# One layer of a hybrid model and two of another on one core: scores between two weight units, transposed values, added squares

## The chip, the core and the metric

The kernel runs on one core of a Trainium2 chip. A core has a matrix engine (TensorE, PE in the rows), VectorE (DVE), ScalarE (ACT), GpSimd (POOL) and SyncE (SP), each with a queue of its own that is worked off in order; they wait for each other through semaphores. Weights come from device memory by DMA. The metric is the time of one execution in microseconds, the median of several runs; less is better.

## What is computed

Two blocks follow each other on 256 tokens of width 1024, everything in fp32. The first has a state-space mixer with a gated norm over two groups of 512 channels, a gated linear attention with a norm over 256 channels a head, cross attention and a gated MLP. The second puts 16 meta tokens in front (272 tokens) and has a stick-breaking attention layer with an MLP, then a recurrent layer with an MLP. The parts that the change touches:

```python
# norms of the first mixer: y over groups of 512 channels, o over heads of 256
y = rmsnorm(y.reshape(Bsz, S, G, SSD_D_INNER // G), norm_g.reshape(G, SSD_D_INNER // G))
o = rmsnorm(o, norm_g).reshape(Bsz, S, GLA_DV)

def _sb_block(q_blk, k, v, q_pos):            # stick-breaking attention, 16 heads of 64
    z = jnp.einsum('bhqd,bhkd->bhqk', q_blk, k).astype(jnp.float32) * (SB_HEAD_DIM ** -0.5)
    causal = k_pos[None, :] < q_pos[:, None]
    log_keep = jnp.where(causal, -jax.nn.softplus(z), 0.0)
    after = lax.cumsum(log_keep, axis=3, reverse=True) - log_keep
    w = jnp.where(causal, jnp.exp(jax.nn.log_sigmoid(z) + after), 0.0)
    return jnp.einsum('bhqk,bhkd->bhqd', w.astype(v.dtype), v)
```

## The kernel before

**Weights.** All weights stream through a ring of four slots in units of 128x1024. For each unit SyncE loads `raw`, ScalarE rounds it to the high part `whi` (`split_hi`), VectorE takes the rest as the low part `wlo` (`split_lo`), and TensorE multiplies both with the high and low part of the activations (`xh`, `xl`): three matmuls for each of eight blocks of 128 channels, 24 a unit (`unit`, lines 438 to 440). A slot's `whi` may be written when TensorE is done with the unit four earlier (`unit_done`), and `wlo` when `whi` is there. Results go to four PSUM banks `acc`, which must have been read (`evacuated`) before the unit four later.

**Queues.** The order of each engine is written out by hand. Nothing is moved by a scheduler: what stands behind a waiting instruction on its engine waits as well.

**Stick-breaking stage.** Two heads make a pair; there are eight pairs, p = 0 to 7, and a ninth set, the tails, for the 16 last queries of all heads. TensorE's loop runs m from 0 to 10. In iteration m it does `sb_after(m-3)` (products of the triangular matrix with the softplus parts `softh` and `softl`, which are added in PSUM), then for m < 8 the query unit 2m and the key unit 2m+1, then `sb_scores(m-1)`: queries by keys into one of two PSUM pairs `z` in the tile `mix`. For m = 8 to 10 a `token_pair` of two value units stands in the place of the query and key units: the activations are the stationary operand and the weights move, so that the values come out token by token; with 128, 128 and 16 tokens it is 72 matmuls. `tail_scores` follows at m = 9. VectorE does in iteration m: `soft_abs(m-2)` (`sp`), `soft_sum(m-2)` (`softp`), `query_rows(2m)` (`sqd`, with the split of the next weights), `soft_lo(m-2)` (`softl`), `key_rows(2m+1)` (`skT`, with a split). ScalarE: `soft_terms(m-2)` (exponential and logarithm on `sp`), `weights(m-3)` (exponential of `z` into `wT`, which frees `z` for the pair after next), `soft_hi(m-2)` (`softh`), two `split_hi`. `sb_scores(p)` waits for `wT_ready` p-1, that is for `weights(p-2)`, since they share `z`.

`token_scales` turns the norm's factors into a column `rtok`, by which `token_scaled` multiplies the values.

**Norms.** In the first mixer's loop over weight units, m = 0 to 59, TensorE sums squares over channels by a matmul with a constant matrix: `st_ssd` at m = 47 over two groups of four blocks, `st_gla0` and `st_gla1` at m = 52 and 54 over two heads of two blocks each. ScalarE makes the squares at m = 44, 45 (`y`) and 50, 51 (`o`).

## Time and profile before

| | us |
|---|---|
| median of three runs | 1232.21 (1231.43 to 1232.97) |
| profiled execution | 1231.64 |
| its span, first to last instruction | 1229.9 |
| TensorE matmuls busy | 1203.1 (98%) |
| VectorE busy | 843.3 (69%) |
| ScalarE busy | 672.1 (55%) |
| mean granted TensorE clock | 0.994 |

The profiled execution is 1.7 us longer than its span. Times in rows count from the span's start. Matmuls overlap, so the distance of two starts is what one costs, not its duration. "Idle" in brackets is how long the engine sat idle before the instruction and what ended that. A matmul in fp32 appears as two instructions.

### The profile page before, as it was taken

How to read it: one execution, taken by the hardware profiler on the slowest of the kernel's cores; microseconds unless marked ns; L12 is line 12 of the kernel's file. 1: busy time of each engine (PE TensorE's matmuls, PEld its weight loads, DVE VectorE, ACT ScalarE, POOL GpSimd, SP SyncE). 2: the span in 40 equal slices, each digit the busy share in tenths (PEclk: the TensorE clock that was granted, in tenths of full speed). 3: DMA queues.
4: the chain of work that ended last, by engine and by line, in shares of the span. 5: the costliest groups of instructions: out<-in, count | busy, mean ns of one | idle time of the engine just before them, and what ended most of it. 6: DMA issues, size and time to landing. Idle time of an engine off the chain costs nothing.

```text
span 1229.9 us, 25642 instructions
## 1 busy us (share of the span) xinstructions
PE 1203.1 (98%) x9675; PEld 1173.0 (95%) x9675; DVE 843.3 (69%) x1271; ACT 672.1 (55%) x1011; POOL 43.5 (4%) x61
## 2 busy tenths in 40 slices
PE   8999999999999999999999999999999999999996
PEld 7999899999999999999988999999999989999996
DVE  6987765888756877776666537666454898766553
ACT  6655545747435656655555326656543686665331
POOL 2002311100000000000100000000000000000000
PEclk9999999999999999999999899999999999999999
DMA  6565434575553565666544224655655536656661
GB/s 217 159 187 161 132 104 125 159 219 182 169 157 122 172 187 185 188 185 188 161 122 123 80 68 141 187 171 177 206 180 174 154 108 186 199 181 185 186 188 51
DMA packets 56776, 197.54 MB, mean 161 GB/s; under 512 B 7152, under 2 KB 9456, under 8 KB 56576
## 3 DMA queue, kind: packets, MB, share of 16 engines
q1 hardware_dynamic: 53856, 192.96, 51.5%
q10 hardware_dynamic: 2848, 3.56, 0.9%
q8 instruction: 52, 0.85, 0.3%
q14 instruction: 20, 0.16, 0.0%
HBM read 195.45 MB, written 1.05 MB: 160 GB/s over the span
## 4 chain that ended last, share of the span: by engine, by line
PE 84%; DVE 9%; ACT 4%; issue 2%; DMA 1%; POOL 0%; ACTq 0%; DVEq 0%; POOLq 0%; SPq 0%
PE acc L438 23%; PE acc L440 23%; PE acc L439 23%; DVE wlo L1486 3%; PE acc L483 2%; PE acc L484 2%; PE acc L485 2%; ACT whi L1017 2%; PE mix L828 1%; DVE sq L1514 1%; PE mix L734 1%; DMA hT<-xT 1%; PE mix L715 1%; PE mix L499 1%; PE mix L609 1%
## 5 line engine op out<-in xcount | busy, mean ns | idle before, releaser
L1017 ACT ACTIVATE whi<-raw 128x1024 fp32r<-128x1024 f32 x366 | 385.3, 1057 | 399.1 <-PE acc L440 345.6
L1486 DVE TENSOR_TENSOR wlo<-raw,whi 128x1024 fp32r<-128x1024 f32 x366 | 447.0, 1224 | 200.8 <-ACT whi L1017 200.3
L438 PE MATMUL acc<-xh,whi 128*128 128x256 f32 (+1 forms) x1664 | 475.1, 286 | 4.5 <-DVE wlo L1486 2.8
L440 PE MATMUL acc<-xh,wlo 128*128 128x256 f32 (+1 forms) x1664 | 471.5, 283 | 0.0
L439 PE MATMUL acc<-xl,whi 128*128 128x256 f32 (+1 forms) x1664 | 471.2, 283 | 0.0
L438 PEld LDWEIGHTS acc<-xh,whi 128*128 128x128 f32 x1664 | 314.1, 189 | 9.3 <-DVE wlo L1486 3.6
L440 PEld LDWEIGHTS acc<-xh,wlo 128*128 128x128 f32 x1664 | 314.5, 189 | 0.0
L439 PEld LDWEIGHTS acc<-xl,whi 128*128 128x128 f32 x1664 | 312.9, 188 | 0.3
L439 PE MATMUL acc<-hl,whi 128*128 128x256 f32 (+1 forms) x688 | 195.4, 284 | 0.0
L438 PE MATMUL acc<-hh,whi 128*128 128x256 f32 (+1 forms) x688 | 195.0, 283 | 0.0
L440 PE MATMUL acc<-hh,wlo 128*128 128x256 f32 (+1 forms) x688 | 194.7, 283 | 0.0
L440 PEld LDWEIGHTS acc<-hh,wlo 128*128 128x128 f32 x688 | 129.9, 189 | 0.0
L439 PEld LDWEIGHTS acc<-hl,whi 128*128 128x128 f32 x688 | 129.4, 188 | 0.0
L438 PEld LDWEIGHTS acc<-hh,whi 128*128 128x128 f32 x688 | 129.1, 188 | 0.0
L438 PE MATMUL acc<-yh,whi 128*128 128x256 f32 (+1 forms) x320 | 91.0, 284 | 3.0 <-DVE yl L2126 1.4
L440 PE MATMUL acc<-yh,wlo 128*128 128x256 f32 (+1 forms) x320 | 90.5, 283 | 0.0
L439 PE MATMUL acc<-yl,whi 128*128 128x256 f32 (+1 forms) x320 | 90.5, 283 | 0.0
L438 PEld LDWEIGHTS acc<-yh,whi 128*128 128x128 f32 x320 | 60.4, 189 | 4.1 <-DVE wlo L1486 3.6
L440 PEld LDWEIGHTS acc<-yh,wlo 128*128 128x128 f32 x320 | 60.5, 189 | 0.0
L439 PEld LDWEIGHTS acc<-yl,whi 128*128 128x128 f32 x320 | 60.1, 188 | 0.0
L2025 DVE SCALAR_TENSOR_TENSOR t<-acc,rstd 128x272 f32<-128x272 f32 (+1 forms) x64 | 27.7, 433 | 31.3 <-PE acc L440 30.8
L483 PE MATMUL acc<-whi,xh 128*128 128x256 f32 (+1 forms) x160 | 45.9, 287 | 0.5 <-DVE wlo L1486 0.5
(350 smaller groups left out, 1423.5 us busy)
## 6 DMA issues: line engine op xcount, KB each, us to landing
raw<-w SPq DMA_DIRECT2D x366, 512.0 KB, 3.6
hT<-xT ACTq DMA_DIRECT2D x2, 512.0 KB, 6.5
mem<-memT ACTq DMA_DIRECT2D x1, 1024.0 KB, 6.8
rgw<-w ACTq DMA_DIRECT2D x2, 512.0 KB, 4.7
out<-hT SPq DMA_DIRECT2D x8, 128.0 KB, 2.0
xdt<-wsmall ACTq DMA_DIRECT2D x1, 192.0 KB, 7.0
pr<-par ACTq DMA_DIRECT2D x1, 114.0 KB, 4.5
hT<-metaT ACTq DMA_DIRECT2D x1, 64.0 KB, 5.8
```

Of the source, the lines that this page charges most:

```text
L438: nc.tensor.matmul(dst, whi[:, slot, n, :], rh, start=first, stop=False)
L439: nc.tensor.matmul(dst, whi[:, slot, n, :], rl, start=False, stop=False)
L440: return nc.tensor.matmul(dst, wlo[:, slot, n, :], rh, start=False, stop=last)
L483: nc.tensor.matmul(dst, ah[:, k, at:at + n], whi[:, s:s + 2, k, :], start=k == 0, stop=False)
L484: nc.tensor.matmul(dst, ah[:, k, at:at + n], wlo[:, s:s + 2, k, :], start=False, stop=False)
L485: last = nc.tensor.matmul(dst, al[:, k, at:at + n], whi[:, s:s + 2, k, :], start=False, stop=k == KB - 1)
L499: last = nc.tensor.matmul(dst[:, 0:T], mean1024[:, :], x[:, 0:T], start=i == 0, stop=i == len(parts) - 1)
L609: last = nc.tensor.matmul(dst[:, 256 * i:256 * i + 256], khk[po:po + CHUNK, c // 2, P * h:P * h + P], vt[po:po + CHUNK, c // 2, 256 * h:25 ...
L715: last = nc.tensor.matmul(mix[:, h % 2, 256 * t:256 * t + 256], xqT[:, 2 * h + i, P * t:P * t + P], xkT[:, 2 * h + i, :], start=i == 0, st ...
L1017: act.activation(whi[:, j, :, :].rearrange("p k c -> p (k c)"), raw[:, j, :], ACT.Copy)\
L1486: dve.tensor_tensor(wlo[:, j, :, :].rearrange("p k c -> p (k c)"), raw[:, j, :], whi[:, j, :, :].rearrange("p k c -> p (k c)").bitcast(F32 ...
L2025: dve.scalar_tensor_tensor(out=t4[:, j, 0:T], in0=acc[:, j, 0:T], scalar=0.0, in1=rstd[:, 0:T], op0=ALU.max, op1=ALU.mult).then_inc(evacua ...
```

## The change

Four edits. In the stick-breaking loop of TensorE the scores of pair m-1 move from behind the key unit to between the query unit and the key unit. On VectorE `softl` moves ahead of the split of the query unit's ring slot. The values are no longer computed token by token: a `value_unit` is an ordinary unit of 24 matmuls over 272 tokens, VectorE multiplies its result by the norm's factor into `svT`, three transposes on TensorE (`values_by_token`) turn it, and ScalarE copies it out (`values_out`); `token_scales` goes. And the squares are added on VectorE before the constant matmul: two additions at m = 46 and one at m = 51, with a new semaphore `n_sums`; `st_ssd` has two matmuls in place of eight, `st_gla0` and `st_gla1` two in place of four.

```diff
-            pool.memset(sv[:, 2, :], 0.0).then_inc(sbzero, 1)
+            pool.memset(svT[:, :, T2:KPAD], 0.0).then_inc(sbzero, 1)
...
+                        pe.wait_ge(n_sums, 2)
                         for grp in range(2):
-                            for b in range(4):
-                                pe.wait_ge(n_sq, 4 * grp + b + 1)
-                                last = nc.tensor.matmul(dst[:, 256 * grp:256 * grp + 256], mean512[:, :],
-                                                        sq[:, 4 * grp + b, 0:T1], start=b == 0, stop=b == 3)
+                            last = nc.tensor.matmul(dst[:, 256 * grp:256 * grp + 256], mean512[:, :],
+                                                    sq[:, 4 * grp, 0:T1], start=True, stop=True)
                         last.then_inc(misc_ready, 1)
...
                         dst = misc_bank(f"st_gla{i}")
+                        pe.wait_ge(n_sums, 3)
                         for hd in range(2):
-                            for vb in range(2):
-                                b = 4 * i + 2 * hd + vb
-                                pe.wait_ge(n_sq, 8 + 2 * i + hd + 1)
-                                last = nc.tensor.matmul(dst[:, 256 * hd:256 * hd + 256], mean256[:, :], sq[:, b, 0:T1],
-                                                        start=vb == 0, stop=vb == 1)
+                            last = nc.tensor.matmul(dst[:, 256 * hd:256 * hd + 256], mean256[:, :],
+                                                    sq[:, 4 * i + 2 * hd, 0:T1], start=True, stop=True)
                         last.then_inc(misc_ready, 1)
...
-            def pair_units(m):
-                for i in range(2):
+            def pair_units(m, halves):
+                for i in halves:
                     if m + i == 0:
...
                         stream_stats("fin1", T1)
-                if m == 1:
-                    token_scales()
-            def token_scales():
-                dst = misc_bank("tok_sb")
-                pe.wait_ge(rstd_ready, 5)
-                for t, (at, n) in enumerate(tiles2):
-                    last = nc.tensor.matmul(dst[0:n, t:t + 1], rstd[:, at:at + n], ident[:, 0:1], start=t == 0, stop=True,
-                                            skip_group_check=True)
...
                 if p == 1:
-                    pe.wait_ge(misc_free, R["tok_sb"] + 1)
+                    pe.wait_ge(misc_free, R["st_fin1"] + 1)
                 if p >= 2:
...
                 dst = mix[:, 3 - p // 2, 256 * (p % 2):256 * (p % 2) + 256]
-                for j in range(2):
-                    pe.wait_ge(evacuated[2 * (p // 2 % 2) + j], OUTS["sv"] // 4 + p // 4 + 1)
+                pe.wait_ge(evacuated[p % 4], OUTS["sv"] // 4 + p // 4 + 1)
                 for h in range(2):
...
+            def value_unit(n):
+                unit("sv", n, n % 4, xh, xl, T2)
+            def values_by_token(n):
+                pe.wait_ge(svT_ready, n + 1)
+                for t in range(3):
+                    last = nc.tensor.transpose(acc[:, n % 4, P * t:P * t + P], svT[:, n % 2, P * t:P * t + P], ident[:, :])
+                last.then_inc(svt_done, 1)
...
                 if m < PAIRS:
-                    pair_units(m)
-                else:
-                    token_pair("sv", 2 * (m - PAIRS), xh, xl, tiles2)
+                    pair_units(m, (0,))
                 if 1 <= m <= PAIRS:
                     sb_scores(m - 1)
-                elif m == PAIRS + 1:
+                if m < PAIRS:
+                    pair_units(m, (1,))
+                else:
+                    n = 2 * (m - PAIRS)
+                    value_unit(n)
+                    if n:
+                        values_by_token(n - 1)
+                    value_unit(n + 1)
+                    values_by_token(n)
+                if m == PAIRS + 1:
                     tail_scores()
             sb_after(PAIRS)
+            values_by_token(5)
             for p in range(4):
...
             tail_out(0)
-            token_pair("sv", 6, xh, xl, tiles2)
+            value_unit(6)
+            value_unit(7)
+            values_by_token(6)
...
             so_part(0, 0, 6)
+            values_by_token(7)
...
+            def values_out(n):
+                act.wait_ge(svt_done, n + 1)
+                act.activation(sv[:, :, P * n:P * n + P], acc[:, n % 4, 0:3 * P].rearrange("p (t c) -> p t c", t=3),
+                               ACT.Copy).then_inc(evacuated[n % 4], 1)
...
                 soft_hi(m - 2)
-                sv_hi(2 * (m - PAIRS))
-                sv_hi(2 * (m - PAIRS) + 1)
+                n = 2 * (m - PAIRS)
+                sv_hi(n)
+                if n:
+                    values_out(n - 1)
+                sv_hi(n + 1)
+                values_out(n)
             weights(PAIRS)
+            values_out(5)
...
             sv_hi(7)
+            values_out(6)
+            values_out(7)
             pairs_out(3)
...
                             dve.tensor_tensor(y[:, b, :], y[:, b, :], sz[:, b, :], ALU.mult).then_inc(n_y, 1)
+                    if m == 46:
+                        dve.wait_ge(n_sq, 8)
+                        grouped = sq[:, :, 0:T1].rearrange("p (g b) t -> p g b t", g=2)
+                        dve.tensor_tensor(grouped[:, :, 0:2, :], grouped[:, :, 0:2, :], grouped[:, :, 2:4, :], ALU.add)\
+                            .then_inc(n_sums, 1)
+                        dve.wait_ge(n_sums, 1)
+                        dve.tensor_tensor(grouped[:, :, 0, :], grouped[:, :, 0, :], grouped[:, :, 1, :], ALU.add)\
+                            .then_inc(n_sums, 1)
+                    if m == 51:
+                        dve.wait_ge(n_sq, 12)
+                        paired = sq[:, :, 0:T1].rearrange("p (h b) t -> p h b t", h=4)
+                        dve.tensor_tensor(paired[:, :, 0, :], paired[:, :, 0, :], paired[:, :, 1, :], ALU.add)\
+                            .then_inc(n_sums, 1)
...
                                              in1=rstd[o_, :], op0=ALU.mult, op1=ALU.mult).then_inc(done, 1)
-                split_lo(UNITS["sqk"][0] + n + 4)
...
                     dve.wait_ge(sbzero, 4)
-                dve.wait_ge(unit_done, UNITS["sv"][0] + 2 * n + 2)
-                token_scaled(sv, 2 * n, (P, P, META))
-                split_lo(UNITS["sv"][0] + 2 * n + 4)
-                split_lo(UNITS["sv"][0] + 2 * n + 5)
+                if n >= 2:
+                    dve.wait_ge(svt_done, n - 1)
+                dve.wait_ge(unit_done, UNITS["sv"][0] + n + 1)
+                dve.tensor_tensor(svT[:, n % 2, 0:T2], acc[:, n % 4, 0:T2], rstd[:, :], ALU.mult).then_inc(svT_ready, 1)
+                split_lo(UNITS["sv"][0] + n + 4)
...
                     soft_lo(m - 2)
+                split_lo(UNITS["sqk"][0] + 2 * m + 4)
                 key_rows(2 * m + 1)
-                if m == 1:
-                    token_scales()
             for m in range(PAIRS, PAIRS + 3):
...
                 soft_lo(m - 2)
-                values(m - PAIRS)
+                values(2 * (m - PAIRS))
+                values(2 * (m - PAIRS) + 1)
                 if m == PAIRS:
...
             tails_lo(0)
-            values(3)
+            values(6)
+            values(7)
             pairs_lo(3)
```

On TensorE around the scores of pair 5, before (L438 to L440 are the matmuls of a weight unit, L813 to L819 the scores, L840 to L848 `sb_after`):

```order
3767 L439 MATMUL acc<-xl,whi 128x272
3768 L440 MATMUL acc<-xh,wlo 128x272
3769 L813 MATMUL mix<-sqd,skT 128x512 [waits evacuated3,wT_ready,evacuated2,sqd_ready]
3770 L815 MATMUL mix<-sqd,skT 128x256
3771 L817 MATMUL mix<-cmask,identb 128x2x128
3772 L819 MATMUL mix<-cmask,identb 128x256
3773 L840 MATMUL mix<-softh,ntri 128x512 [waits softl_ready]
3774 L842 MATMUL mix<-softh,nones 128x2x128
```

and of the change, where they are L440 to L442, L801 to L807 and L828 to L836:

```order
3740 L441 MATMUL acc<-xl,whi 128x272
3741 L442 MATMUL acc<-xh,wlo 128x272
3742 L801 MATMUL mix<-sqd,skT 128x512 [waits evacuated3,wT_ready,evacuated2,sqd_ready]
3743 L803 MATMUL mix<-sqd,skT 128x256
3744 L805 MATMUL mix<-cmask,identb 128x2x128
3745 L807 MATMUL mix<-cmask,identb 128x256
3746 L440 MATMUL acc<-xh,whi 128x272 [waits evacuated1,lo_ready]
```

The scores have moved ahead of the key unit, with the same waits, and `sb_after` of the next iteration no longer follows on them.

On TensorE at the end of the last key unit, the scores of pair 7, before (L483 to L485 are the last matmuls of a token pair):

```order
3907 L484 MATMUL acc<-wlo,xh 16x256
3908 L485 MATMUL acc<-whi,xl 16x256
3909 L813 MATMUL mix<-sqd,skT 128x512 [waits evacuated3,wT_ready,evacuated2,sqd_ready]
3910 L815 MATMUL mix<-sqd,skT 128x256
3911 L817 MATMUL mix<-cmask,identb 128x2x128
```

and of the change:

```order
3827 L442 MATMUL acc<-xh,wlo 128x272
3828 L828 MATMUL mix<-softh,ntri 128x512 [waits softl_ready]
3829 L830 MATMUL mix<-softh,nones 128x2x128
3830 L836 MATMUL mix<-softh,ntri 128x256
3831 L828 MATMUL mix<-softl,ntri 128x512
3832 L830 MATMUL mix<-softl,nones 128x2x128
3833 L836 MATMUL mix<-softl,ntri 128x256
3834 L801 MATMUL mix<-sqd,skT 128x512 [waits evacuated3,wT_ready,evacuated2,sqd_ready]
3835 L803 MATMUL mix<-sqd,skT 128x256
```

The scores of pair 7 stood behind a token pair; now they stand directly behind `sb_after(5)`.

On VectorE in one iteration of the same loop, before:

```order
599 L1957 TENSOR_SCALAR sp<-mix 128x768 [waits head_ready]
600 L1963 SCALAR_TENSOR_TENSOR softp<-mix,sp 128x768 [waits sb_act]
601 L1944 SCALAR_TENSOR_TENSOR sqd<-acc,rstd 64x272 [waits unit_done]
602 L1944 SCALAR_TENSOR_TENSOR sqd<-acc,rstd 64x272
603 L1486 TENSOR_TENSOR wlo<-raw,whi 128x1024 [waits hi_ready]
604 L1968 TENSOR_TENSOR softl<-softp,softh 128x768 [waits softh_ready]
605 L1951 TENSOR_TENSOR skT<-acc,rstd 128x272 [waits unit_done]
606 L1486 TENSOR_TENSOR wlo<-raw,whi 128x1024 [waits hi_ready]
```

and of the change:

```order
600 L1980 TENSOR_SCALAR sp<-mix 128x768 [waits head_ready]
601 L1986 SCALAR_TENSOR_TENSOR softp<-mix,sp 128x768 [waits sb_act]
602 L1968 SCALAR_TENSOR_TENSOR sqd<-acc,rstd 64x272 [waits unit_done]
603 L1968 SCALAR_TENSOR_TENSOR sqd<-acc,rstd 64x272
604 L1991 TENSOR_TENSOR softl<-softp,softh 128x768 [waits softh_ready]
605 L1506 TENSOR_TENSOR wlo<-raw,whi 128x1024 [waits hi_ready]
606 L1974 TENSOR_TENSOR skT<-acc,rstd 128x272 [waits unit_done]
607 L1506 TENSOR_TENSOR wlo<-raw,whi 128x1024 [waits hi_ready]
```

`softl` and the first of the two splits have changed places.

## Rows read from the trace of the kernel before

**Rows 1.** The page, part 1: busy time, share of the span, instructions of each engine.

```profile
PE 1203.1 (98%) x9675; PEld 1173.0 (95%) x9675; DVE 843.3 (69%) x1271; ACT 672.1 (55%) x1011; POOL 43.5 (4%) x61
```

**Rows 2.** Timeline of TensorE, one round: start, duration, instruction, [idle before].

```profile
626.68 0.50 PE L840 MATMUL mix<-softh,ntri 128*128 128x512 f32 x1 [0.42 <-DVE softl L1968]
...
627.73 0.28 PE L438 MATMUL acc<-xh,whi 128*128 128x272 f32 x1
...
633.77 1.02 PE L813 MATMUL mix<-sqd,skT 128*128 128x512 f32 x2
...
635.85 0.51 PE L840 MATMUL mix<-softh,ntri 128*128 128x512 f32 x1 [0.41 <-DVE softl L1968]
```

**Rows 3.** Timeline of VectorE, from one `sp` to the next.

```profile
637.32 0.95 DVE L1957 TENSOR_SCALAR sp<-mix 128x768 uint32<-128x768 uint32 x1
640.06 0.96 DVE L1963 SCALAR_TENSOR_TENSOR softp<-mix,sp 128x768 f32<-128x768 f32 x1 [1.79 <-ACT sp L1312]
...
645.36 1.22 DVE L1486 TENSOR_TENSOR wlo<-raw,whi 128x1024 fp32r<-128x1024 f32 x1
646.49 0.95 DVE L1957 TENSOR_SCALAR sp<-mix 128x768 uint32<-128x768 uint32 x1
```

**Rows 4.** Timeline of ScalarE in the same round.

```profile
639.93 0.80 ACT L1322 ACTIVATE wT<-mix 128x768 f32<-128x768 f32 x1
```

**Rows 5.** Timeline of TensorE at the end of key unit 3, m = 1.

```profile
616.36 0.63 PE L796 MATMUL mix<-ident,rstd 128*128 128x1 f32 x6
616.92 1.12 PE L813 MATMUL mix<-sqd,skT 128*128 128x512 f32 x2
...
618.45 0.37 PE L438 MATMUL acc<-xh,whi 128*128 128x272 f32 x1
```

**Rows 6.** Timeline of VectorE there.

```profile
616.56 0.44 DVE L1951 TENSOR_TENSOR skT<-acc,rstd 128x272 f32<-128x272 f32 x1 [0.65 <-PE acc L440]
617.71 1.23 DVE L1486 TENSOR_TENSOR wlo<-raw,whi 128x1024 fp32r<-128x1024 f32 x1 [0.71 <-ACT whi L1017]
```

**Rows 7.** Timeline of ScalarE there.

```profile
616.62 1.06 ACT L1017 ACTIVATE whi<-raw 128x1024 fp32r<-128x1024 f32 x1 [1.97 <-PE acc L440]
```

**Rows 8.** Timeline of TensorE: ends of a token pair's neighbours, and a pair's start.

```profile
684.31 0.28 PE L848 MATMUL mix<-softl,ntri 128*128 128x256 f32 x1
...
692.92 7.71 PE L828 MATMUL mix<-sqd,skT 128*128 128x32 f32 x48
...
702.35 0.41 PE L483 MATMUL acc<-whi,xh 128*128 128x256 f32 x1
```

**Rows 9.** Timeline of TensorE in the first mixer: eight transposes.

```profile
84.73 1.04 PE L556 MATMUL mix<-ident,xc 128*128 128x128 f32 x8
```

**Rows 10.** Timeline of VectorE at m = 8.

```profile
678.63 0.96 DVE L1968 TENSOR_TENSOR softl<-softp,softh 128x768 fp32r<-128x768 f32 x1 [0.91 <-ACT softh L1318]
...
685.71 1.73 DVE L1924 RECIPROCAL rstdh<-rtf 128x256 f32<-128x256 f32 x1
```

**Rows 11.** Timeline of TensorE at `st_ssd` (L680) and `st_gla1` (L691).

```profile
188.51 3.61 PE L680 MATMUL mix<-sq,mean 128*128 128x256 f32 x16
191.77 0.47 PE L438 MATMUL acc<-xh,whi 128*128 128x256 f32 x1
...
219.12 1.99 PE L691 MATMUL mix<-sq,mean 128*128 128x256 f32 x8 [0.90 <-ACT khk L1199]
```

**Rows 12.** Timeline of VectorE at m = 46.

```profile
187.02 1.23 DVE L1486 TENSOR_TENSOR wlo<-raw,whi 128x1024 fp32r<-128x1024 f32 x1 [0.72 <-ACT whi L1017]
```

**Rows 13.** Timeline of ScalarE at m = 51.

```profile
209.65 1.13 ACT L1194 ACTIVATE sq<-xdt 128x512 f32<-128x512 f32 x2
```

**Rows 14.** Stretches: busy us of each engine, granted clock, DMA share, GB/s.

```profile
694.00:696.00 2.00, 2.00 (x20) 2.00 (x19) 2.00 (x3) 1.18 (x2) 0.00 (x0) 0.93 0.00 0
705.00:706.00 1.00, 1.00 (x7) 1.00 (x7) 0.51 (x1) 0.46 (x1) 0.00 (x0) 0.52 0.00 0
1224.00:1226.00 2.00, 0.00 (x0) 0.00 (x0) 2.00 (x6) 0.00 (x0) 0.00 (x0) 0.70 0.39 134
```

More of the change, by code:

```diff
@@ L94 @@
         "st_gla0", "st_gla1", "st_mem", "st_xattn", "pt0", "pt1", "pt2", "pt3",
[1 row of a table removed]
+        "st_ffn", "st_sb", "st_fin1", "st_mlp0", "st_lru", "st_mlp1", "st_fin2"]
 R = {name: n for n, name in enumerate(MISC)}
@@ L258, in blocks_kernel @@
         sv = sb("sv", [P, 3, D], stack=s4)
+        svT = sb("svT", [P, 2, KPAD], stack=s4)
         sp = sb("sp", [P, ZC], stack=s4)
@@ L308, in blocks_kernel @@
         n_sq, n_r, n_y, o_step = sem("n_sq"), sem("n_r"), sem("n_y"), sem("o_step")
+        n_sums = sem("n_sums")
         yh_ready, yl_ready, merged = sem("yh_ready"), sem("yl_ready"), sem("merged")
@@ L316, in blocks_kernel @@
         tail_done, sqd_ready = sem("tail_done"), sem("sqd_ready")
-        tok_ready = sem("tok_ready")
+        svT_ready, svt_done = sem("svT_ready"), sem("svt_done")
         both_ready, meta_ready, metah_ready, metal_ready, metasq_ready, sqb_ready, sumb_ready = [sem(n) for n in
@@ L515, in operand @@
                 return xl_ready, KB * OPER[norm]
-            tiles1, tiles2 = [(0, P), (P, P)], [(0, P), (P, P), (2 * P, META)]
+            tiles1 = [(0, P), (P, P)]
             def small_products():
@@ L787, in pair_units @@
                         stream_stats("fin1", T1)
-                if m == 1:
-                    token_scales()
-            def token_scales():
-                dst = misc_bank("tok_sb")
-                pe.wait_ge(rstd_ready, 5)
-                for t, (at, n) in enumerate(tiles2):
-                    last = nc.tensor.matmul(dst[0:n, t:t + 1], rstd[:, at:at + n], ident[:, 0:1], start=t == 0, stop=True,
-                                            skip_group_check=True)
-                last.then_inc(misc_ready, 1)
             def sb_scores(p):
@@ L1561, in token_scaled @@
                 c = 128 * m
-                if len(tiles) == 3:
-                    dve.tensor_scalar(dst[0:META, 2, c:c + 256], acc[0:META, m % 4, 256:512], rtok[0:META, 2:3], None,
-                                      ALU.mult)
                 for t in range(2):
@@ L1926, in stream_rms @@
                 dve.wait_ge(rstd_ready, norms[0])
-            def token_scales():
-                dve.wait_ge(misc_ready, R["tok_sb"] + 1)
-                dve.tensor_copy(rtok[:, 0:2], mix[:, MISCB, 0:2]).then_inc(tok_ready, 1)
-                dve.tensor_copy(rtok[0:META, 2:3], mix[0:META, MISCB, 2:3]).then_inc(misc_free, 1)
             inverse_rms("sb", T2)
```

1 row of the table MISC is left out of this document.

## The prediction

> **What bounds the kernel now.** I read the page first: TensorE is busy in 98% of the span [rows 1], so the time is what TensorE has to issue, plus the little it waits. A part that only frees VectorE or ScalarE changes nothing until it ends a TensorE wait, and a part that makes TensorE wait costs its whole length. Then I read the timeline of TensorE through the stick-breaking stage. In rounds m = 3 to 7 it repeats every 9.17 us [rows 2]: `sb_after(m-3)` takes 1.05 us (626.68 to 627.73), two weight units take 6.04 us (627.73 to 633.77), the scores follow, and then TensorE waits 0.41 us for `softl`. The scores cost 1.53 us of issue (616.92 to 618.45, [rows 5]). So TensorE has 1.05 + 6.04 + 1.53 = 8.62 us of work in a round. The 0.41 to 0.43 us wait stands six times in this stage. Last I read VectorE and ScalarE in the same rounds [rows 3, 4], because both serve the weight splits and the softplus in one queue each, and the edit reorders who waits for whom.
>
> **Where the scores stand, and what they need.** `sb_scores(m-1)` overwrites the PSUM pair that `weights(m-3)` reads, so it waits for `wT_ready`. In ScalarE's queue `weights(m-3)` stands behind the two softplus steps of pair m-2, and these wait for `soft_abs(m-2)`, which stands in VectorE's queue behind `key_rows(2m-1)` and its weight split. Now there are two units (6.04 us) between `sb_after(m-3)` and the scores. `sp` starts at 637.32 [rows 3], `wT` starts at 639.93 and takes 0.80 [rows 4]: it is ready 3.41 us after `sp` starts, at 640.73. `sb_after` started at 635.85 [rows 2] and with one unit behind it would be through at 635.85 + 1.05 + 3.02 = 639.92, earlier than 640.73. The second unit is what hides `wT` today; the change takes it out of that place and puts it behind the scores.
>
> **The new round.** A loop closes that was open before: `sp` of a pair, `wT` (3.41 us), scores (0.06 to wake TensorE, 1.53), key unit (3.02), its evacuation `skT`, the split of the next weights, next `sp`. The end of that loop has its own rows: TensorE leaves the key unit at 616.36 [rows 5], `skT` starts at 616.56 (0.20 later), and the split waits for ScalarE's `whi`, which itself may start only when this unit is done (616.62, [rows 7]); so `wlo` starts at 617.71, 1.15 after `skT` [rows 6]. From the split to the next `sp` it is 1.13 (645.36 to 646.49, [rows 3]). Sum: 3.41 + 0.06 + 1.53 + 3.02 + 0.20 + 1.15 + 1.13 = **10.50 us** a round, against 8.62 us of TensorE work. TensorE then waits 1.88 us before the scores of pairs 2 to 6: **+9.4 us** in five rounds. The low part of softplus ahead of the weight split does what it says: five of the six waits for `softl` go, 5 x 0.42 = **-2.1 us** (the first round, where nothing has fallen behind yet, keeps its own). But `softl` isn't on the new loop, and so it can't shorten it.
>
> **The scores of pair 7.** In iteration m = 8 there is no query unit, and the scores follow directly on `sb_after(5)`. Before, a pair of value units of 8.4 us stood between. Count from the end of the last key unit: 0.20 + 1.15 + 1.13 to `sp`, 3.41 to `wT`, 0.06: 5.95 us, of which `sb_after(5)` covers 1.05. TensorE waits **+4.9 us**.
>
> **Values.** A token pair costs 684.31 + 0.12 to 692.92, 8.49 us [rows 8], for 72 matmuls. In its place: two units (6.04) and six transposes. Eight transposes take 1.04 us [rows 9], 0.13 each, so 0.78. Saved 8.49 - 6.04 - 0.78 = 1.67 a pair, four pairs: **-6.7 us**. ScalarE gets eight copies of 128x384 out of PSUM, each below the 0.80 that `wT` takes for 768 columns [rows 4], and VectorE loses its twelve token scalings for eight multiplications of the kind of `skT`, 0.44 [rows 6]; both engines have idle time there (0.91 of it stands in [rows 10]), and I cost them at nothing. Without that cover it would be 0.5 us a copy, 4 us at most. But `values_by_token(2)` stands right behind unit 3 and ahead of the tail scores, and its `svT` comes on VectorE behind `softl` of pair 7. From the end of value unit 1: TensorE has 0.33 + 1.05 + 3.02 + 0.33 + 3.02 = 7.75 us to do. VectorE has evacuation and split (0.20 + 1.15 + 1.13), the reciprocal of 1.73 [rows 10], `sp` to `softp` 2.74 (637.32 to 640.06, [rows 3]), `softp` to `softl` 1.87 (0.96 and then 0.91 of waiting for `softh`, [rows 3, 10]), `softl` 0.93, the multiplication 0.44, the wake-up 0.06: 10.25. TensorE waits **+2.5 us**. `token_scales` goes, with 616.36 to 616.92: **-0.6 us** [rows 5].
>
> **Added squares.** `st_ssd` drops from 16 instructions in 3.26 us (188.51 to 191.77, [rows 11]) to 4, 0.85 us. But the two additions start on VectorE after the split that starts at 187.02 [rows 12]: 1.13 + 1.25 + 0.70, so the sums are there at 190.1 and TensorE waits 1.6 us. The first adds 1024 columns as the split does (1.23), the second half of that. 0.85 + 1.6 in place of 3.26: -0.8. At `st_gla0` four instructions go (-0.8), but it now waits for ScalarE's squares of m = 51, whose pair starts at 209.65 and takes 1.13 [rows 13], and for 1.2 us of VectorE behind: ready at 212.1, while TensorE got there at 210.65; +0.7 net. `st_gla1` keeps its 0.90 wait for ScalarE [rows 11] and loses 0.8. Together **-0.8 us**; bounds -3.5 (if no sum is waited for) and +1.
>
> **TensorE's clock.** The granted clock was halved once in the middle of the run: it goes down in 694 to 696 and comes back in 705 to 706 [rows 14]. Ahead of the fall stood the tail scores, matmuls of 32 columns, since 692.92. It also fell at the end: matmuls had stopped by 1221.4, and within 1224 to 1226 the mean is 0.70 [rows 14]. The first of these stretches stays, since the tail scores do. The 4.9 us wait is new and holds no matmul at all, so I expect a second low stretch behind it. Before, dense matmuls ran from 702.35 [rows 8] to about 705.9 at half clock before it was lifted, 3.6 us in which half was lost: **+1.8 us**. Bounds 0 (no fall) and 3.6 (twice as long, or the fall ahead of the tail scores earlier as well, since 2.5 us of waiting now stand before them).
> The Trainium skill, TensorE: Matmul & The Clock Gate, section "HAM oscillation", says that an array left idle in a wait between bursts is throttled again and starts the next burst cold. The end of this trace agrees (1224 to 1226 above). By that rule the term is there; by a reading in which only sparse matmuls, as the tail scores, bring the fall it would be 0 and the time 1.8 us lower.
>
> **Sum.** +9.4 + 4.9 + 2.5 - 2.1 - 6.7 - 0.6 - 0.8 = +6.6, with the clock +1.8: **+8.4 us**. The profiled execution took 1231.64 us (span 1229.9 and 1.7 around it), so 1240.0 by its own time; the median of the runs shown, 1232.21, is 0.6 above it: **1240.6 us**.
>
> **Rivals.** (A) The round is not closed as I say: weights are ready when the scores need them, and TensorE stays the only bound. Then the waits are not there and 6.7 + 2.5 + 0.6 + 0.8 = 10.6 us go: 1221.6 us, faster. For it: TensorE's share of 98%, and the instruction count falls. Against it: the 3.41 us of [rows 3, 4] and the order of the queues, both plain. It decides where `wT` of pair m-3 is ready less than 4.07 us after `sb_after(m-3)` starts. Chance 0.08. (B) The waits are there, but about 60% as large, since a round starts from a VectorE that had slack (a shorter `sp`-to-`wT` step or a split that finds its `whi` early); 16.8 x 0.6 = 10.1 of waits against 10.2 saved: 1232 us. Chance 0.07. (C) The clock: a second and a longer first low stretch, 3.6 us in place of 1.8, and each wait 10% longer (1.7), since every switch between kinds of matmul costs about 0.1: 8.4 + 3.5 = 11.9, 1244.1 us. Chance 0.15. The forecast holds 0.70, from 1237.0 (waits 10% shorter, no second fall) to 1242.5.
>
> **Range and chances.** 1235 to 1244.5 leaves out A, most of B and the far end of C. A measurement of this kernel can tell about 0.2% (2.5 us) from no change. Faster than 1229.7: A and a little of B, 0.09. Within: the rest of B, 0.06. Slower: 0.85.
>
> **What would show it.** Right: in the timeline, rounds of 10.5 us between the `sp` instructions; TensorE's first score matmul with 1.9 us of idle released by ScalarE's `wT`, five times, and once 4.9 us; no idle ahead of `sb_after` but in the first round; 2.5 us ahead of the third group of transposes, released by `svT`; a second low stretch of the clock behind the 4.9 us. TensorE's busy time falls by about 10 us while the span grows. Wrong: rounds of 8.6 us (A); a wait for `wT` well under 1 us (B); a clock that stays full behind the long wait takes 1.8 off. The squares are wrong if TensorE reaches `st_ssd` after the second addition, which would make them -3 alone.

## The result and the profile after

The changed kernel takes **1244.44 us** (median of 5 runs, 1244.09 to 1245.14) against 1232.21 (1231.43 to 1232.97): ratio 1.0103, 95% interval 1.0089 to 1.0117. It is slower, as forecast, but by 12.2 us and not by 8.4. The profiled execution took 1244.44, with a span of 1242.7. Page and list of waits of the changed kernel, TensorE's rows; a wait's columns are us in total, times, longest:

```profile
PE 1198.7 (96%) x9577; PEld 1169.3 (94%) x9577; DVE 845.5 (68%) x1268; ACT 675.6 (54%) x1019; POOL 41.5 (3%) x61
```

TensorE does less work than in [rows 1] and is busy for a smaller share of a longer span. But its busy time fell by 4.4 us only, where the forecast had about 10: matmuls at a low clock are busy for longer. Where it waits:

```profile
PE mix L801 <- ACT wT L1330: 14.6, 6, 4.9
PE acc L872 <- DVE svT L2001: 2.5, 1, 2.5
PE mix L681 <- DVE sq L1765: 1.6, 1, 1.6
PE mix L690 <- DVE sq L1770: 1.4, 1, 1.4
PE mix L828 <- DVE softl L1991: 0.4, 1, 0.4
```

The first row is the new one: six waits ahead of the scores, five of about 1.9 us and one of 4.9, all released by ScalarE's `wT`. The last one is what is left of the six waits of [rows 2]. Timelines of one round at the full clock, TensorE, then VectorE and ScalarE (start, duration, instruction, idle before and its releaser); they answer to [rows 2, 3, 4]:

```profile
643.58 1.10 PE L801 MATMUL mix<-sqd,skT 128*128 128x512 f32 x2 [1.92 <-ACT wT L1330]
...
648.20 0.39 PE L828 MATMUL mix<-softh,ntri 128*128 128x512 f32 x1
...
654.24 1.10 PE L801 MATMUL mix<-sqd,skT 128*128 128x512 f32 x2 [1.92 <-ACT wT L1330]
```

```profile
648.40 0.44 DVE L1974 TENSOR_TENSOR skT<-acc,rstd 128x272 f32<-128x272 f32 x1 [1.59 <-PE acc L442]
649.55 1.23 DVE L1506 TENSOR_TENSOR wlo<-raw,whi 128x1024 fp32r<-128x1024 f32 x1 [0.71 <-ACT whi L1025]
650.69 0.95 DVE L1980 TENSOR_SCALAR sp<-mix 128x768 uint32<-128x768 uint32 x1
653.43 0.96 DVE L1986 SCALAR_TENSOR_TENSOR softp<-mix,sp 128x768 f32<-128x768 f32 x1 [1.78 <-ACT sp L1320]
```

```profile
651.68 0.84 ACT L1318 ACTIVATE sp<-sp 128x768 f32<-128x768 f32 x1 [2.16 <-DVE sp L1980]
652.55 0.84 ACT L1320 ACTIVATE sp<-sp 128x768 f32<-128x768 f32 x1
653.30 0.79 ACT L1330 ACTIVATE wT<-mix 128x768 f32<-128x768 f32 x1
```

This is the loop of the forecast, closed: the key unit ends at 648.20, `skT` follows at 648.40, the split at 649.55, `sp` at 650.69, `wT` ends at 654.09, and the scores that follow start at 654.24. The round is 654.24 - 643.58 = 10.66 us (forecast 10.50; 9.17 before). Of the 0.16 too little, 0.09 is the step from the end of `wT` to the scores (0.15 us, forecast 0.06) and 0.07 is scores and key unit (643.58 to 648.20, 4.62 us, forecast 4.55).

What the forecast had too small is the clock. The granted clock has two levels in these rows, full (1.00) and half (0.50); a value between is a stretch that held both. Stretches of the changed kernel from one pair's scores to the next (us, TensorE busy with its count, granted clock, DMA share, GB/s):

```profile
631.34:643.58 12.24, 10.32 (x61) 0.86 0.34 97
643.58:654.24 10.66, 8.74 (x61) 1.00 0.33 100
654.24:664.90 10.66, 8.74 (x60) 1.00 0.33 98
664.90:677.09 12.19, 10.27 (x61) 0.86 0.28 88
677.09:687.74 10.65, 5.72 (x36) 0.95 0.35 98
687.74:698.33 10.59, 10.59 (x58) 0.73 0.01 2
708.72:717.21 8.49, 8.49 (x52) 0.61 0.47 125
```

Of the first four rows two are 1.6 and 1.5 us longer than the others, with the same instructions and nearly the same wait (2.00 against 1.92 us at 631.34), and these two have a mean clock of 0.86. The sixth row is the stretch behind the 4.9 us wait, the last one the tail scores. The scores and the two units behind that wait take 10.34 us:

```profile
687.74 2.05 PE L801 MATMUL mix<-sqd,skT 128*128 128x512 f32 x2 [4.93 <-ACT wT L1330]
...
698.08 0.49 PE L872 MATMUL acc<-ident,svT 128*128 128x128 f32 x3
```

The low clock at the tail scores isn't new. It is the same in both traces, 13 us of which have a mean clock of 0.61 (before, then after); in the changed kernel it only starts earlier against them:

```profile
694.00:707.00 13.00, 13.00 (x73) 0.61 0.25 81
709.00:722.00 13.00, 13.00 (x72) 0.61 0.30 82
```

Both traces cut at the same instructions (the first matmul of `sb_after`, and the end of the span):

| stretch | before | after | difference | forecast |
|---|---|---|---|---|
| start to m = 3 (squares, token scales) | 626.68 | 625.11 | -1.6 | -1.4 |
| m = 3 to m = 8, five rounds | 45.87 | 56.60 | +10.7 | +7.3 |
| m = 8 to m = 9 (pair 7, first values) | 10.86 | 16.62 | +5.8 | +5.0 |
| m = 9 to m = 10 (values, tail scores) | 17.09 | 18.88 | +1.8 | +0.8 |
| m = 10 to the end (two pairs of values) | 529.40 | 525.49 | -3.9 | -3.3 |
| sum | 1229.9 | 1242.7 | +12.8 | +8.4 |

The tail scores took 7.58 us before (692.92 to 700.50, clock 0.69) and take 8.49 now, and the units behind them lose as much less: 0.9 us of the last two differences has only moved from the last row to the one above it.

### The profile page after: what moved, and what is told of

It is laid out like the page before. It is cut to its first block, busy times and chain, and to the rows that moved or that the text cites. A ratio compares the mean times of both kernels' runs of the same rounds, so it can differ in the third digit from the quotient of the medians.

```text
span 1242.7 us, 25454 instructions
## 1 busy us (share of the span) xinstructions
PE 1198.7 (96%) x9577; PEld 1169.3 (94%) x9577; DVE 845.5 (68%) x1268; ACT 675.6 (54%) x1019; POOL 41.5 (3%) x61
## 4 chain that ended last, share of the span: by engine, by line
PE 84%; DVE 8%; ACT 5%; issue 2%; DMA 1%; POOL 0%; ACTq 0%; DVEq 0%; POOLq 0%; SPq 0%
PE acc L440 24%; PE acc L442 24%; PE acc L441 24%; DVE wlo L1506 3%; ACT whi L1025 2%; PE acc L485 1%; PE acc L486 1%; PE acc L487 1%; PE mix L801 1%; PE mix L816 1%; DVE sq L1534 1%; PE mix L733 1%; DVE sp L1980 1%; PE mix L714 1%; ACT sp L1318 1%
## 5 line engine op out<-in xcount | busy, mean ns | idle before, releaser
L440 PE MATMUL acc<-xh,whi 128*128 128x256 f32 (+1 forms) x1728 | 496.6, 287 | 3.6 <-DVE wlo L1506 1.9
L442 PE MATMUL acc<-xh,wlo 128*128 128x256 f32 (+1 forms) x1728 | 491.5, 284 | 0.0
L441 PE MATMUL acc<-xl,whi 128*128 128x256 f32 (+1 forms) x1728 | 491.4, 284 | 0.0
L440 PEld LDWEIGHTS acc<-xh,whi 128*128 128x128 f32 x1728 | 328.3, 190 | 8.7 <-DVE wlo L1506 2.7
L442 PEld LDWEIGHTS acc<-xh,wlo 128*128 128x128 f32 x1728 | 328.3, 190 | 0.0
L441 PEld LDWEIGHTS acc<-xl,whi 128*128 128x128 f32 x1728 | 327.0, 189 | 0.3
L440 PE MATMUL acc<-hh,whi 128*128 128x256 f32 (+1 forms) x688 | 195.0, 283 | 0.0
L442 PE MATMUL acc<-hh,wlo 128*128 128x256 f32 (+1 forms) x688 | 194.7, 283 | 0.0
L442 PEld LDWEIGHTS acc<-hh,wlo 128*128 128x128 f32 x688 | 129.9, 189 | 0.0
L440 PEld LDWEIGHTS acc<-hh,whi 128*128 128x128 f32 x688 | 129.1, 188 | 0.0
L440 PE MATMUL acc<-yh,whi 128*128 128x256 f32 (+1 forms) x320 | 91.2, 285 | 3.1 <-DVE yl L2151 1.4
L442 PE MATMUL acc<-yh,wlo 128*128 128x256 f32 (+1 forms) x320 | 90.5, 283 | 0.0
L440 PEld LDWEIGHTS acc<-yh,whi 128*128 128x128 f32 x320 | 60.4, 189 | 4.2 <-DVE wlo L1506 3.6
L442 PEld LDWEIGHTS acc<-yh,wlo 128*128 128x128 f32 x320 | 60.5, 189 | 0.0
L1396 ACT ACTIVATE hh<-t 128x272 f32 (+1 forms) x64 | 27.2, 426 | 8.4
```

What stands on the lines that cost most here:

```text
L440: nc.tensor.matmul(dst, whi[:, slot, n, :], rh, start=first, stop=False)
L441: nc.tensor.matmul(dst, whi[:, slot, n, :], rl, start=False, stop=False)
L442: return nc.tensor.matmul(dst, wlo[:, slot, n, :], rh, start=False, stop=last)
L1396: act.activation(blk(hh, 4 * i + j, 0, T), t4[:, j, 0:T], ACT.Copy).then_inc(hh_ready, 1)
```

## The experiments

Each edit is made to the kernel that its heading or text names. Each time is the median of four or more executions, but for one, which is named; each trace is of one execution.

**1. The order undone.** The changed kernel, its scores behind both units again:

```diff
                 if m < PAIRS:
-                    pair_units(m, (0,))
-                if 1 <= m <= PAIRS:
-                    sb_scores(m - 1)
-                if m < PAIRS:
-                    pair_units(m, (1,))
+                    pair_units(m, (0, 1))
                 else:
...
+                if 1 <= m <= PAIRS:
+                    sb_scores(m - 1)
                 if m == PAIRS + 1:
                     tail_scores()
```

> The changed kernel with one part undone: the scores of a head pair stand again behind both weight units of their round. My theory is that this order alone made the loss, by a loop (scores, DVE's softplus chain, ScalarE's order, weights, next scores) and by the low clock behind its waits. Then the 14.6 us in which PE waits for wT ahead of mix and the low clock stretches in the rounds (about 6 us) go, what is left is the gain of the other parts: 1232.2 less 2.1 (wait for softl), 6.7 (values), 0.6 (token scales), 0.8 (squares), and about 1.0 back for a wait ahead of the transposes of value block 2, so about 1223, round of 8.6 to 8.7 us. Rival: the extra low clock comes from the value units and their transposes, not from the waits; then it stays and the time is about 1228. Second rival: the softplus chain itself has become longer by the earlier softl, then a round stays over 10 us and the time stays at 1240 or more.

Measured: **1220.99 us** (1220.46 to 1223.91), ratio to before 0.9917 (0.9904 to 0.9931). Wherever TensorE stands in the stage, it is now this (list of waits), and from 600 to 680 us the clock is full:

```profile
PE acc L872 <- DVE svT L1999: 0.9, 1, 0.9
```

```profile
600.00:680.00 80.00, 79.19 (x567) 1.00 0.45 133
```

On top of the other edits the order costs 1244.4 - 1221.0 = 23.4 us; without it the rest of the change is a gain of 11.2.

**2. The order alone**, in the kernel before (the same lines the other way round).

> The kernel before with one part of the change alone: the scores of a pair between the two weight units. By the loop, a round takes 10.66 us as in the changed kernel, against 9.04 before: five of them, +8.1. The wait ahead of the scores of pair 7 is 4.9, and the low clock stretches of the rounds cost about 6: 1232.2 + 8.1 + 4.9 + 6 = 1251, worse than the whole change. If the clock is not the waits' doing, 1245. Rival: the order is harmless by itself and becomes harmful only with the earlier softl or the value units (ScalarE's copies): then 1232 to 1235.

Measured: **1250.88 us** (1248.33 to 1251.20), ratio 1.0148 (1.0133 to 1.0164); forecast 1251. Its list of waits:

```profile
PE mix L813 <- ACT wT L1324: 13.4, 6, 4.9
PE mix L840 <- DVE softl L1970: 2.6, 1, 2.6
```

The loop needs neither the earlier `softl` nor the value units. From one `sb_after` to the next its rounds take 9.63, 12.31, 10.64, 12.20 and 10.66 us, so here too two of five have low clock:

```profile
638.15:650.46 12.31, 10.39 (x63) 0.86 0.35 120
650.46:661.10 10.64, 8.72 (x62) 1.00 0.20 54
```

In the kernel before, the order costs 18.7 us, 4.7 less than in experiment 1. About that much (4.2, experiment 5) is what the earlier `softl` is worth where the loop is open: behind the closed loop the round is 10.66 with it and without it. The rival that makes it harmless by itself is out by 16 us.

**3. The loop opened on ScalarE.** The changed kernel with its order of scores:

```diff
-                if m >= 2:
-                    soft_terms(m - 2)
                 if m >= 3:
                     weights(m - 3)
+                if m >= 2:
+                    soft_terms(m - 2)
```

> The changed kernel, with its order of scores, and one change on ScalarE alone: the weights of a pair (wT) are formed ahead of the softplus terms of the next pair. If the loop is what makes PE wait, and ScalarE's order is what closes it, the waits of 1.92 us ahead of the scores of pairs 2 to 6 go, the 4.93 us one ahead of pair 7 falls to about 1, and the clock falls no more often than before: 1244.4 - 9.6 - 3.9 - 6 = 1225, round of 8.6 to 8.8 us. Rival: DVE's chain of a pair (sp, softp, softl) is the limit, not ScalarE's order: then the waits only move to softl and the time stays within 3 us of 1244.

Measured: **1226.14 us** (1223.68 to 1228.20), ratio 0.9946 (0.9932 to 0.9960); forecast 1225. List of waits, and three rounds (the two calls change places in the loop for m = 8 to 10 as well):

```profile
PE mix L801 <- ACT wT L1330: 1.1, 1, 1.1
```

```profile
637.39:645.88 8.49, 8.49 (x63) 1.00 0.37 120
645.88:654.37 8.49, 8.49 (x62) 1.00 0.42 123
654.37:662.87 8.50, 8.50 (x63) 1.00 0.40 127
```

Two exchanged calls on an engine that is busy 54% of the time take 18 us off. The rounds have the full clock. At the tail scores this execution (1228.2, the slowest of the five) has more low clock than the kernel before, where it was 0.61 over 13 us; the expectation had excluded that:

```profile
688.00:704.00 16.00, 16.00 (x84) 0.57 0.23 67
```

The experiment shows that the link of the loop is ScalarE's queue, where `weights(m-3)` stood behind softplus steps that it doesn't need; VectorE's chain isn't the limit. It also gives TensorE's work in a round without a wait: 8.49 us, where the forecast had 8.62.

**4. TensorE kept busy in its waits.** The changed kernel, with matmuls whose result the next unit of the bank overwrites:

```diff
+            def filler(count, j, turns):
+                pe.wait_ge(evacuated[j], turns)
+                for n in range(count):
+                    nc.tensor.matmul(acc[:, j, 0:256], nones[:, :], xh[:, 0, 0:256], start=True, stop=True)
             def sb_scores(p):
+                if p == PAIRS - 1:
+                    filler(36, 0, OUTS["sv"] // 4)
+                elif p >= 2:
+                    filler(13, (2 * p + 3) % 4, (OUTS["sqk"] + 2 * p + 3) // 4)
...
+                    if n == 2:
+                        filler(17, 0, OUTS["sv"] // 4 + 1)
                     values_by_token(n)
```

> The changed kernel with matmuls added whose result nobody reads (they are overwritten by the next unit of their bank): 13 ahead of the scores of each of pairs 2 to 6, 36 ahead of those of pair 7, 17 ahead of the transposes of value block 2, each of 256 columns, 0.12 us apart. They fill the time in which PE waits there and change nothing else, so the waits' length in time stays and PE is busy in them. If the low clock stretches in the rounds come from PE standing still, they go and their cost with them: 1244.4 - 6 = 1238.4, granted clock of 1.00 through the five rounds, each 10.66 us. If the clock has another cause, the stretches stay and the time is 1244.4 or, with fillers that run over at the low clock, up to 1246.

Measured: **1237.70 us** (1236.44 to 1240.92), ratio 1.0057 (1.0043 to 1.0071). Four rounds, and the timeline at one of their waits:

```profile
632.40:643.07 10.67, 10.28 (x73) 1.00 0.37 109
643.07:653.72 10.65, 10.28 (x73) 1.00 0.31 98
653.72:664.38 10.66, 10.28 (x73) 1.00 0.32 100
664.38:675.05 10.67, 10.29 (x74) 1.00 0.35 99
```

```profile
653.72 1.10 PE L811 MATMUL mix<-sqd,skT 128*128 128x512 f32 x2 [0.37 <-ACT wT L1342]
```

The rounds keep their 10.66 us, as the loop wants it, and every one of them is at 1.00. More work by 118 matmuls, and 6.7 us less time. The rival with another cause of the clock had 1244.4 or more. So the waits without matmuls are the cause of the low clock in the rounds. The 6.7 isn't its price alone, though. Against the trace of the change the five rounds take 3.1 us less (53.5) and the stage with pair 7 2.7 less (13.93): 5.8 behind the waits. The stage with the tail scores is 2.9 shorter as well, since the low clock is shorter there (mean 0.89 from 698 to 714, against 0.61 over 13 us), and the stretch up to m = 3 is 1.1 longer; the execution in the trace is the fastest of the five, 1236.44.

**5. to 7. The other parts alone**, each in the kernel before: `softl` ahead of the split, the values by channel without token scales, the added squares. The second and third take their hunks from the diff of the change; of each the core:

```diff
                                              in1=rstd[o_, :], op0=ALU.mult, op1=ALU.mult).then_inc(done, 1)
-                split_lo(UNITS["sqk"][0] + n + 4)
...
                     soft_lo(m - 2)
+                split_lo(UNITS["sqk"][0] + 2 * m + 4)
                 key_rows(2 * m + 1)
```

```diff
-                    token_pair("sv", 2 * (m - PAIRS), xh, xl, tiles2)
+                    n = 2 * (m - PAIRS)
+                    value_unit(n)
+                    if n:
+                        values_by_token(n - 1)
+                    value_unit(n + 1)
+                    values_by_token(n)
```

```diff
+                        pe.wait_ge(n_sums, 2)
                         for grp in range(2):
...
+                            last = nc.tensor.matmul(dst[:, 256 * grp:256 * grp + 256], mean512[:, :],
+                                                    sq[:, 4 * grp, 0:T1], start=True, stop=True)
```

> The kernel before with one part of the change alone: on DVE the low part of softplus (softl) stands ahead of the split of the first weight unit's low part. PE waited six times 0.42 us for softl, 2.5 in all. My theory: these waits go and nothing else becomes late, 1232.2 - 2.5 = 1229.7. Rival: the split that now stands behind softl comes late for its unit (a wait ahead of the first unit of a round), or the waits are taken up by a stretch of low clock that starts elsewhere: then 1232.

> The kernel before with one part of the change alone: the values formed by channel in eight units, scaled on DVE and transposed on PE, and the token scales gone. By the sum of the forecast a pair of values costs 6.82 instead of 8.49 (four pairs, -6.7), the token scales 0.6, and a wait of about 1 us stands ahead of the transposes of value block 2, as in the run with the order undone, where it was 0.90: 1232.2 - 6.7 - 0.6 + 1.0 = 1225.9. Rival: the gain in the values is smaller than the sum says and part of what the run with the order undone gained came from softl or the squares: then 1228 or more.

> The kernel before with one part of the change alone: the squares of the statistics added on DVE, so that PE multiplies a quarter (SSD) and a half (GLA) as often. The sum: PE's 3.61 us become 1.10 behind a wait of 1.6, its two of 1.9 become 1.10 each, one behind a wait of 1.4 in place of the one of 0.9 the other had: -0.8, 1231.4. Rival: PE's waits are longer than the work saved, because DVE takes up the adding at a time at which it is itself late: 1232.5 or more. It is near what five rounds can tell; the trace with its waits must decide.

Measured: `softl` alone **1227.69 us** (1226.39 to 1229.02), ratio 0.9964 (0.9951 to 0.9978); values alone **1225.78** (1225.06 to 1227.05), 0.9953 (0.9940 to 0.9967); squares alone **1230.69** (1229.76 to 1232.00), 0.9991 (0.9982 to 1.0000). Against their 1231.86 of before these are -4.2, -6.1 and -1.2, together -11.4: the 11.2 that experiment 1 left. The squares are at the edge of what the runs tell; their two waits stand in the trace as forecast, 1.6 and 1.4.

`softl` brought more than the 2.5 us of its waits. The timeline of the kernel before, from the last score matmul to the wait, and of this kernel at the same place and a round later, say why:

```profile
635.17 0.27 PE L819 MATMUL mix<-cmask,identb 128*128 128x256 bf16 x1
635.85 0.51 PE L840 MATMUL mix<-softh,ntri 128*128 128x512 f32 x1 [0.41 <-DVE softl L1968]
```

```profile
635.22 0.27 PE L819 MATMUL mix<-cmask,identb 128*128 128x256 bf16 x1
635.24 0.48 PE L840 MATMUL mix<-softh,ntri 128*128 128x512 f32 x1
...
643.74 0.48 PE L840 MATMUL mix<-softh,ntri 128*128 128x512 f32 x1
```

Without a wait a matmul starts while the one ahead of it is still running, here 0.02 us behind its start. With the wait it starts 0.68 behind. The shown idle time of 0.41 leaves out the overlap that is lost. The round agrees: 643.74 - 635.24 = 8.50 us in place of 9.17. Six such waits are 6 x 0.68 = 4.1 us, the measured 4.2.

**8. The tail scores woven into value units**, on the kernel of experiment 1 (one product of 32 columns, `tail_scores(1)`, behind each product of the second half of unit 3 and the first half of unit 4):

```diff
+            def woven_unit(n, first, stop):
...
+                for k in range(KB):
+                    if first <= k < stop and len(tail_products) == 3 * PAIRS:
+                        pe.wait_ge(wT_ready, PAIRS - 1)
...
+                        if first <= k < stop:
+                            tail_scores(1)
```

> Built on the changed kernel with the order of scores undone (1221.0): the 24 products of the tail scores no longer stand in one row but one behind each of 12 products in the second half of value unit 3 and of 12 in the first half of value unit 4. In the run with the order undone they took 8.5 us, most of it at a granted clock of 0.50, and the softplus terms behind them made nobody wait. Theory: the clock falls there since PE has only these small products to do for several us; woven between full products it stays at 1.00 and the 4.9 us lost to the low clock in that stretch go, as does the 0.9 us wait ahead of them: 1216 with a second wait of up to 1 for the low part of the last softplus. Rival: the clock falls all the same, because the small products are as many and only spread: then 1220 to 1221, and since the last softplus chain starts no earlier, a wait of 2 to 4 us ahead of its use makes it 1223.

Measured: **1218.57 us** (1215.80 to 1218.88), ratio 0.9887 (0.9871 to 0.9902). Two stretches of experiment 1, then the same of this kernel:

```profile
686.00:696.00 10.00, 10.00 (x50) 0.53 0.35 107
706.00:716.00 10.00, 10.00 (x96) 1.00 0.16 54
```

```profile
686.00:696.00 10.00, 10.00 (x85) 1.00 0.35 107
706.00:716.00 10.00, 10.00 (x72) 0.83 0.00 0
```

The same small products no longer bring the clock down where they are spread between full ones:

```profile
682.96 0.37 PE L880 MATMUL acc<-xl,whi 128*128 128x272 f32 x1
683.17 0.30 PE L817 MATMUL mix<-sqd,skT 128*128 128x32 f32 x2
```

But it falls later, behind the next row of small products (the tails' outputs), so that only half of the expected gain arrived, 2.4 us.

**9. and 10. Late sums, and woven outputs.** On the kernel of 8, `st_ssd`, `st_gla0` and `st_gla1` in the middle of the next weight unit; and on that, the outputs of the tails between the products of value unit 6:

```diff
+            middle = {48: ssd_sums, 53: lambda: gla_sums(0), 55: lambda: gla_sums(1)}
...
-                        unit(phase, n, n % 4, xh, xl, T1)
+                        unit(phase, n, n % 4, xh, xl, T1, mid=middle.get(m))
```

```diff
-            tail_out(0)
-            value_unit(6)
+            unit_with(6, out_piece)
```

> The kernel with the woven tail scores (1218.6), with one more edit: PE multiplies the added squares not at the end of weight units 47, 52 and 54, but in the middle of units 48, 53 and 55, 1.5 us later, while DVE is adding. PE's waits of 1.6 and 1.4 us ahead of these products were all that kept the added squares from being worth their saved work. Theory: both go and nobody else comes late, since DVE's reciprocal behind the first one starts some 4 us behind the products: 1218.6 - 3.0 = 1215.6. Rival: ScalarE, which takes the roots ahead of its weight splits, stands 1.5 us longer and PE waits for the next weight unit instead: 1218.6 or a little more.

> The kernel of the run beside it, and in addition the 18 products of 32 columns that make the tails of the first six pairs are woven one by one between the products of value unit 6, where they stood in one row of 4.4 us, behind which the granted clock was 0.87 and 0.79 in two stretches of 5 us (1.7 us lost). Theory: the clock stays up, -1.7, and their own time stays: 1213.9 if the late sums bring their 3.0. Rival: this low stretch comes from the pairs' own products ahead of them (64 columns wide in the weights) and stays, or the readers of the tails come later and make PE wait: no gain over the run beside it.

> The kernel with the woven tail scores and the late sums once more, for a look alone. Its profiled execution took 1217.8 us and had a low granted clock from 705 to 720 us worth about 3.4 us, while four executions without a profile took 1212.8 to 1214.8. If this low stretch comes in some executions and not in others, this look shows either 1213 to 1214 with a clock of 1.00 there, or again 1217 to 1218 with the stretch. If it comes in all of them and the difference is the profiler's, a time near 1217.8 with the stretch says nothing new, and a time near 1213 with the stretch in it speaks against the clock as the cause.

Measured: late sums **1213.22 us** (1212.82 to 1217.79), ratio 0.9849 (0.9836 to 0.9862); with woven outputs **1213.31** (1212.88 to 1214.21), 0.9850 (0.9836 to 0.9863); a single further execution of the first of the two 1217.03. The late sums brought 5.4 us where 3.0 were expected: besides the waits of 1.6 and 1.4, the 0.9 ahead of `st_gla1` went as well, and one of 0.4 came:

```profile
PE mix L624 <- ACT kt L1135: 0.4, 1, 0.4
```

That is 3.5 us of shown waits. The remaining 2 us are within the spread of the two kernels. By the medians the second edit brought nothing. By the traces it did what it should (the first row is late sums, the second with woven outputs), while both profiled executions of the first have the low stretch and take 1217 to 1218:

```profile
706.00:716.00 10.00, 10.00 (x58) 0.66 0.00 0
```

```profile
706.00:716.00 10.00, 10.00 (x83) 1.00 0.30 78
```

That isn't the only difference between the two. Late sums have a second low stretch near the start of the execution (first row), woven outputs have none there (second row), and the edits don't reach that place:

```profile
14.00:20.00 6.00, 4.69 (x25) 0.72 0.61 229
14.00:20.00 6.00, 4.30 (x32) 1.00 0.51 179
```

Of the 4.9 us between these two traces, 3.2 stand behind the last `sb_after` and 1.7 ahead of m = 3. A low stretch at 14 to 20 us stands in 7 of the 13 traces, a place that no edit here reaches: in those of experiments 4 to 9 and of the further execution.

My reading is that each of these stretches comes in some executions of the kernel of late sums and not in others, since four without a profile took 1212.8 to 1214.8; no trace of such a short execution exists, so it stays open. The woven outputs spread over 1.3 us and the late sums over 5; with five executions each it isn't shown that the weave did this. Both are 18.8 to 18.9 us, 1.5%, faster than the kernel before, and 31 faster than the change.

## Why the prediction was wrong in its size

**Right: the loop.** Five waits of 1.92 to 2.00 us (forecast 1.88), a round of 10.66 (10.50), released by `wT`; closed by ScalarE's order (experiment 3) and by nothing else in the change (experiments 1 and 2). **Right: pair 7**, 4.93 us against 4.9; **the wait for `svT`**, 2.5 against 2.5; the squares' 1.6; the one wait for `softl` that stays. **Right: the gains.** Values and token scales, less the wait of the value transposes: -6.1 alone. The squares -1.2 alone, forecast -0.8 (its own three parts add up to -0.9). The -2.1 for `softl` holds only as a part of the sum, which counts the new waits from 8.62 us of work; by itself it is worth 4.2 without the loop, and next to nothing with it.

**Wrong: the step "TensorE's clock"**, a term of +1.8 with bounds of 0 and 3.6. It counted one new low stretch, behind the wait of 4.9 us, and put the bound at twice that. I had costed the five waits of 1.9 us at their length alone. Two of the rounds that hold them have a clock of 0.86: 12.43 and 12.18 us from one `sb_after` to the next against 10.66, +1.8 and +1.5. Behind the long wait the scores and two units took 10.34 us where they take 1.50 + 6.04 at the full clock: +2.8, so that the one stretch that was counted was sized too low as well. Together 6.1 by the trace; in experiment 4, with matmuls in the waits, these stages are 5.8 shorter. This is 4.3 us more than the term and above its upper bound. It takes the time to the very end of the range (1244.44 by the median, just inside 1244.5; 1244.9 by the ratio, just outside).

**Wrong and hidden: two terms that nearly cancel.** The round was 0.16 us longer than forecast, +0.8 in five. The work of a round was taken as 8.62 plus a wait of 0.42, 9.04, where [rows 2] show 9.17 from one to the next (-0.7). By experiments 3 and 5 these 9.17 are 8.49 of work and 0.68 for the wait: a wait costs about 0.25 us more than its shown idle time. The parts outside the rounds came out within 0.3 us of their terms each, and as their sum, once the 0.9 that only moved is set off. 4.3 + 0.8 - 0.7 = 4.4, what lies between forecast and trace.

**The rivals.** A (no waits) and B (60% of them) are out by the waits alone. C had the cause in part and the time nearly, 1244.1, but this is luck: it had a longer first stretch and waits 10% longer, where the first stretch stayed as long as before, the waits came out as forecast, and new stretches stood in the rounds.

## What to carry to other kernels

Before moving an operation forward on one engine, follow its releaser through the queue of the engine that makes it: it is the order there, not the work, that closes a loop, and exchanging two calls on the half-idle ScalarE was worth 18 us of the 23 that the move had cost. Price a recurring wait on TensorE at its shown idle time, plus the lost overlap (0.25 us here), plus half the length of the low clock stretches that it brings. Where the wait can't be removed, matmuls that fill it pay for themselves (experiment 4). A row of small matmuls goes between full ones (experiment 8). Before a low stretch is put down to an edit, look whether it also stands where the edit doesn't reach. Read a round's length from start to start in the timeline, not as a sum of busy and idle.

## What the runs showed of the hardware

- The granted clock fell to 0.5 behind waits as short as 1.9 us (1.92 and 2.00) that recur every 10.66 us, but in two rounds of five, with the same instructions and nearly the same waits in all; experiment 2 has two of five as well. With matmuls in the waits it was 1.00 in all rounds. Waits of 0.4 us every 9.17 us ([rows 2]) never brought it down. What decides which of the rounds it is, no run here shows.
- It also fell where TensorE was never idle but had only matmuls of 32 columns for several us (before, 692.92 to 700.50: busy throughout, mean clock 0.69, 0.50 from 696 on). Woven one for one between matmuls of 272 columns they left it at 1.00. Full and small product together then took 0.35 us, a full one alone takes 0.13.
- A wait that the trace shows as 0.41 us costs 0.68 (rounds of 9.17 against 8.49).
- Low stretches also come and go between traces where no edit reaches: one at 14 to 20 us stands in 7 of 13, with a mean clock of 0.72 there against 1.00.
